# An expert stage rebuilt: batched gathers, expert outputs summed in PSUM, and weight splitting shared between three engines

## The reference

```python
combine = einsum('bske,bsk->bse', one_hot(expert_id, 16), p_g * top_p)
out = zeros_like(h)
for e in range(16):
    he = silu(h @ w_gate[e]) * (h @ w_up[e])        # 1024 -> 512
    out = out + combine[..., e:e + 1] * (he @ w_down[e])   # 512 -> 1024
x = x + out
```

## Time and profile before

| what | us |
|---|---|
| median of three runs | 1732.67 |
| the profiled execution: span from first to last instruction | 1733.3 |
| TensorE busy | 1584.7 (91%) |
| VectorE busy | 894.1 (52%) |
| ScalarE busy | 728.9 (42%) |
| GpSimd busy | 416.0 (24%) |

### The profile page before, as it was taken

One profiled execution on the slowest core, in us unless ns is written; L12 is line 12 of the kernel. 1 busy time (PEld: TensorE's weight loads), 2 busy tenths in 40 slices (PEclk: granted clock), 3 DMA queues, 4 the chain that ended last, 5 costly groups with the idle time before them and its releaser, 6 DMA issues. The chain is left out here.

```text
span 1733.3 us, 20738 instructions
## 1 busy us (share of the span) xinstructions
PE 1584.7 (91%) x6276; PEld 1251.4 (72%) x6276; DVE 894.1 (52%) x1403; ACT 728.9 (42%) x1033; POOL 416.0 (24%) x461
## 2 busy tenths in 40 slices
...
PEclk8998899997778788888879998999958888888877
...
GB/s 204 123 159 133 49 49 243 146 23 136 186 261 226 234 259 219 241 250 233 153 126 136 133 97 91 56 194 146 98 122 205 234 242 242 242 242 242 240 244 38
DMA packets 58345, 298.82 MB, mean 172 GB/s; under 512 B 4016, under 2 KB 8224, under 8 KB 45728
## 3 DMA queue, kind: packets, MB, share of 16 engines
...
## 5 line engine op out<-in xcount | busy, mean ns | idle before, releaser
L988 ACT ACTIVATE w_hi<-ring 128x1024 fp32r<-128x1024 f32 x424 | 424.9, 1057 | 27.9 <-PE bank L522 26.3
L1908 DVE TENSOR_TENSOR w_lo<-ring,w_hi 128x1024 fp32r<-128x1024 f32 x320 | 377.5, 1222 | 82.2 <-ACT w_hi L988 81.2
L1440 POOL TENSOR_TENSOR w_lo<-ring,w_hi 128x1024 fp32r<-128x1024 f32 x64 | 152.0, 2375 | 688.0 <-ACT w_hi L988 688.0
L863 PE MATMUL bank<-pick,h 128*128 128x64 f32 x1024 | 250.5, 419 | 3.7 <-DVE pick L1900 3.7
L863 PEld LDWEIGHTS bank<-pick,h 128*128 128x128 f32 x1024 | 249.3, 334 | 5.3 <-DVE pick L1900 3.9
L457 PE MATMUL bank<-ring,hT 128*128 128x512 f32 (+2 forms) x576 | 217.3, 538 | 4.0 <-ACT hT L1023 2.2
L892 PE MATMUL bank<-w_hi,ga 128*128 128x512 f32 x512 | 210.0, 410 | 3.8 <-DVE ga L1913 3.0
L893 PE MATMUL bank<-w_lo,ga 128*128 128x512 f32 x512 | 203.4, 397 | 0.0
L457 PEld LDWEIGHTS bank<-ring,hT 128*128 128x128 f32 x576 | 113.3, 199 | 101.7 <-issue 96.3
L939 PE MATMUL bank<-w_hi,hidT 128*128 128x512 f32 x256 | 142.1, 555 | 5.4 <-DVE hidT L1938 5.4
L940 PE MATMUL bank<-w_lo,hidT 128*128 128x512 f32 x256 | 133.6, 522 | 0.0
...
## 6 DMA issues: line engine op xcount, KB each, us to landing
ring<-in_w_e_gate SPq DMA_DIRECT2D x32, 2048.0 KB, 7.7
ring<-in_w_e_up SPq DMA_DIRECT2D x32, 2048.0 KB, 7.7
ring<-in_w_e_down SPq DMA_DIRECT2D x32, 2048.0 KB, 7.7
ring<-in_w_in SPq DMA_DIRECT2D x24, 2048.0 KB, 8.1
ring<-in_w_ckv SPq DMA_DIRECT2D x4, 2048.0 KB, 8.2
ring<-in_w_branch SPq DMA_DIRECT2D x4, 2048.0 KB, 10.4
ring<-in_w_out SPq DMA_DIRECT2D x4, 2048.0 KB, 10.4
ring<-in_w_cq SPq DMA_DIRECT2D x2, 2048.0 KB, 13.2
```

What stands on the lines that cost most here:

```text
L863: ins = mm(dst, h[:, tb, k::KD], pick[:, tb, 0, :], start=(tb == 0), stop=(tb == TB - 1))
L988: return A(dst, src, ACT.Copy, **kw)
L1440: g.tensor_tensor(w_lo[:, n % RP, :], ring[:, e_slot[j], 3 * PIECE:4 * PIECE], w_hi[:, n % RP, :].bitcast(F32), ALU.subtract).then_inc(sem ...
L1908: v.tensor_tensor(w_lo[:, n % RP, :], ring[:, e_slot[j], i * PIECE:i * PIECE + PIECE], w_hi[:, n % RP, :].bitcast(F32), ALU.subtract).then ...
```

## The change

The expert stage is rebuilt in these parts, the code of all other stages stays, but for the place of `hT` in SBUF and a few merged semaphores:

- **Gather.** The normed tokens `h` are split once a layer into `hs_hi` and `hs_lo` (ACT, DVE), and `pick` is made once for all 16 experts, as fp32r. One gather step is 4 matmuls with 256 columns (4 experts by 64 places) for one k of 8; the steps of the first group stand ahead of the turns, those of the next group are spread over the turns of the present one, two a turn. Both parts come out of the same bank, and one cast writes them to `ga` (ACT for even k, DVE for odd).
- **Fold.** ACT copies rows 64 to 127 of a gate or up bank to rows 0 to 63 of `gul` (`gl`, `ul`), DVE adds the other half from PSUM. silu and product are taken there, before the transposes: 4 matmuls by `ident` with 64 columns. The product also takes the token's weight `cw`, which comes out of the same two matmuls as `pickT` (`idc` holds the identity and the weights as high and low parts).
- **Scatter.** All experts are accumulated in four banks (`ACC`), and `x` is added to once at the end of the stage. `pickT` has two buffers; GpSimd copies its rows 0 to 63 to rows 64 to 127.
- **Splitting.** Pieces 0 to 2 of every chunk are ACT's and DVE's. Piece 3 of every chunk is GpSimd's alone, the cast to `w_hi` and the subtraction. SyncE waits for `w_lo` and `w_lo_p` itself.
- **Order.** The turns are written out one after the other, without a loop. The first gate chunk is split, and `hs_hi` and `hs_lo` are made, before the routing. The parameters of the next layer are issued by GpSimd behind its first piece.

```diff
+PER_TURN = dict(w_hi=9, w_lo=9, w_hi_p=3, w_lo_p=3, w_used=12, ga_mm=2, ga_ev_a=1, ga_ev_v=1,
+                pickT_mm=1, pickT=1, pickT_p=1, gu_cp=2, gu_sum=2, act_gate=1, hid=1,
+                hidT_mm=1, hidT_hi=1, hidT_lo=1, y_mm=1, y_hi=2, y_lo=2)
+PER_PASS = dict(pick=1, sc_mm=4, x_acc=4)
...
+GROUP = 4
+GROUPS = N_EXP // GROUP
+IDC = P + 2 * N_EXP
...
+SHARED_PIECES = (0, 1, 2)
...
+                def gather(b, g, k):
+
+                    for a, tok in enumerate((hs_hi, hs_lo)):
                         for tb in range(TB):
+                            ins = mm(bank[b][:, a * 256:a * 256 + 256], tok[:, tb, k, :],
+                                     pick[:, tb, GROUP * g:GROUP * g + GROUP, :].rearrange("p e c -> p (e c)"),
+                                     start=(tb == 0), stop=(tb == TB - 1))
...
+                            b = ACC[nh * 2 + tb]
+                            to = pickT[:, e % 2, tb * P:tb * P + P]
+                            mm(bank[b][:], to, y_hi[:, c], start=(e == 0), stop=False)
+                            ins = mm(bank[b][:], to, y_lo[:, c], start=False, stop=(e == N_EXP - 1))
+                            if e == N_EXP - 1:
+                                ins.then_inc(sem("sc_mm"), 1)
...
+                def turn(p, e):
+                    g, i = e // GROUP, e % GROUP
+
+                    pe.wait_ge(sem("ga_ev_a"), turns_before("ga_ev_a", l, p, 0) + min(N_EXP, GROUP * (g + 1)))
+                    pe.wait_ge(sem("ga_ev_v"), turns_before("ga_ev_v", l, p, 0) + min(N_EXP, GROUP * (g + 1) + i))
+                    widen(p, e, 0)
+
+                    if e > 0:
+                        pe.wait_ge(sem("y_lo"), turns_before("y_lo", l, p, e - 1) + 1)
+                    for tb in range(TB):
+                        ins = mm(bank[2][0:CAP, tb * IDC:tb * IDC + IDC], pick[:, tb, e, :], idc[:, tb, :],
+                                 start=True, stop=True)
+                    ins.then_inc(sem("pickT_mm"), 1)
+                    widen(p, e, 1)
+
+                    if g + 1 < GROUPS:
+                        pe.wait_ge(sem("gu_sum"), turns_before("gu_sum", l, p, e) + 1)
+                        gather(0, g + 1, 2 * i)
+                    if e > 0:
+                        scatter(p, e - 1)
+                    if g + 1 < GROUPS:
+                        pe.wait_ge(sem("ga_ev_a"), turns_before("ga_ev_a", l, p, 0) + GROUP * (g + 1) + i + 1)
+                        gather(0, g + 1, 2 * i + 1)
+
+                    pe.wait_ge(sem("hid"), turns_before("hid", l, p, e) + 1)
+                    q.settle()
...
+                        ins = tr(bank[1][:, t * CAP:t * CAP + CAP], hid[:, t::4], ident[0:CAP, 0:CAP])
+                    ins.then_inc(sem("hidT_mm"), 1)
...
+                def gathered(p, b, g, k):
+
+                    act.wait_ge(sem("ga_mm"), turns_before("ga_mm", l, p, 0) + g * KD + k + 1)
+                    copy(ga[:, g % 2, k].rearrange("p e a c -> p a e c"),
+                         bank[b][:].rearrange("p (a e c) -> p a e c", a=2, e=GROUP)).then_inc(sem("ga_ev_a"), 1)
...
+                    copy(gl, bank[0][CAP:P, :]).then_inc(sem("gu_cp"), 1)
...
+                    copy(pickT[0:CAP, e % 2, :].rearrange("p (t n) -> p t n", t=TB), both[:, :, 0:P])
+                    copy(cw_parts[0:CAP], both[:, :, P + e:IDC:N_EXP], accum_out=cw[0:CAP, :]).then_inc(sem("pickT"), 1)
+                    pieces(p, e, 2, (0,))
+                    act.wait_ge(sem("gu_sum"), turns_before("gu_sum", l, p, e) + 1)
+                    A(gl, gl, ACT.Silu).then_inc(sem("act_gate"), 1)
...
+                    copy(ul, bank[1][CAP:P, :]).then_inc(sem("gu_cp"), 1)
+                    if g + 1 < GROUPS:
+                        gathered(p, 0, g + 1, 2 * i)
...
+                pieces(0, 0, 0, SHARED_PIECES)
+                for tb in range(TB):
+                    act.wait_ge(sem("h_gained"), l * PER["h_gained"] + tb + 1)
+                    copy(hs_hi[:, tb], h[:, tb, :].rearrange("p (f k) -> p k f", k=KD)).then_inc(sem("hs_hi"), 1)
...
+                    pool.wait_ge(sem("w_used"), turns_before("w_used", l, p, e) + n + 1)
+                    q.settle()
+                    src = ring[:, s_, 3 * PIECE:4 * PIECE]
+                    g.tensor_copy(w_hi[:, n % RP, :], src).then_inc(sem("w_hi_p"), 1)
+                    pool.wait_ge(sem("w_hi_p"), turns_before("w_hi_p", l, p, e) + j + 1)
+                    q.settle()
+                    g.tensor_tensor(w_lo[:, n % RP, :], src, w_hi[:, n % RP, :].bitcast(F32),
+                                    ALU.subtract).then_inc(sem("w_lo_p"), 1)
+
+                def turn(p, e):
                     piece(p, e, 1)
+                    pool.wait_ge(sem("w_lo_p"), turns_before("w_lo_p", l, p, e) + LO_P_BIAS + 2)
+                    q.settle()
+                    pool.wait_ge(sem("pickT"), turns_before("pickT", l, p, e) + 1)
+                    q.settle()
+                    g.tensor_copy(pickT[CAP:P, e % 2, :], pickT[0:CAP, e % 2, :]).then_inc(sem("pickT_p"), 1)
+                    pool.wait_ge(sem("pickT_p"), turns_before("pickT_p", l, p, e) + 1)
+                    q.settle()
                     piece(p, e, 2)
...
+                piece(0, 0, 0)
+                for tb in range(TB):
+                    ins = g.tensor_copy(idc[:, tb, 0:P], ident[:])
+                ins.then_inc(sem("idc"), 1)
+                layer_parameters(bass.ds((L - 1) - l, 1))
...
+                pieces(0, 0, 0, SHARED_PIECES)
+                for tb in range(TB):
+                    dve.wait_ge(sem("hs_hi"), l * PER["hs_hi"] + tb + 1)
+                    v.tensor_tensor(hs_lo[:, tb], h[:, tb, :].rearrange("p (f k) -> p k f", k=KD),
+                                    hs_hi[:, tb].bitcast(F32), ALU.subtract).then_inc(sem("hs_lo"), 1)
...
+                def choose(p):
+
+                    first = p * N_EXP
                     for tb in range(TB):
+                        at = place[:, tb, first:first + N_EXP] if isinstance(first, int) else place[:, tb, bass.ds(first, N_EXP)]
+                        ins = v.tensor_tensor(pick[:, tb], bc(slot_no[:], [P, N_EXP, CAP]),
+                                              bc(at.unsqueeze(2), [P, N_EXP, CAP]), ALU.is_equal)
                     ins.then_inc(sem("pick"), 1)
...
+                def turn(p, e):
+                    g, i = e // GROUP, e % GROUP
+                    pieces(p, e, 1, SHARED_PIECES)
+                    dve.wait_ge(sem("gu_cp"), turns_before("gu_cp", l, p, e) + 1)
+                    v.tensor_tensor(gl, bank[0][0:CAP, :], gl, ALU.add).then_inc(sem("gu_sum"), 1)
+                    pieces(p, e, 2, (0,))
+                    dve.wait_ge(sem("gu_cp"), turns_before("gu_cp", l, p, e) + 2)
+                    v.tensor_tensor(ul, bank[1][0:CAP, :], ul, ALU.add).then_inc(sem("gu_sum"), 1)
+                    dve.wait_ge(sem("gu_sum"), turns_before("gu_sum", l, p, e) + 2)
...
+                    dve.wait_ge(sem("pickT"), turns_before("pickT", l, p, e) + 1)
+                    v.scalar_tensor_tensor(out=hid, in0=ul, scalar=cw[0:CAP, :], in1=gl,
+                                           op0=ALU.mult, op1=ALU.mult).then_inc(sem("hid"), 1)
+                    pieces(p, e, 2, (1,))
+                    if g + 1 < GROUPS:
+                        gathered(p, 0, g + 1, 2 * i + 1)
                     dve.wait_ge(sem("hidT_hi"), turns_before("hidT_hi", l, p, e) + 1)
+                    v.tensor_tensor(hidT[:, :, 1, :], bank[1][:, 0:4 * CAP].rearrange("p (t c) -> p t c", t=4),
+                                    hidT[:, :, 0, :].bitcast(F32), ALU.subtract).then_inc(sem("hidT_lo"), 1)
+                    pieces(p, e, 2, (2,))
+                    if e < N_EXP - 1:
+                        pieces(p, e + 1, 0, SHARED_PIECES)
...
+                        v.tensor_tensor(xv, bank[ACC[n]][:], xv, ALU.add).then_inc(sem("x_acc"), 1)
```

More of the change, by code:

```diff
@@ L73, in split_piece_used @@
     return LAST_USE[SPLIT[n // 4]] if n % 4 == 3 else ("dw_used", 3 * (n // 4) + n % 4 + 1)
-PER_TURN = dict(split=3, w_hi=12, w_lo=10, w_lo_p=2, w_used=12, pick=1, pickT_mm=1, pickT=1, ga_mm=1, ga_hi=1,
-                ga_lo=1, gu_sb=2, guT_mm=2, act_gate=1, hid=1, hidT_hi=1, hidT_lo=1,
-                y_mm=1, y_hi=2, y_lo=2, sc_mm=4, x_acc=4)
+PER_TURN = dict(w_hi=9, w_lo=9, w_hi_p=3, w_lo_p=3, w_used=12, ga_mm=2, ga_ev_a=1, ga_ev_v=1,
+                pickT_mm=1, pickT=1, pickT_p=1, gu_cp=2, gu_sum=2, act_gate=1, hid=1,
+                hidT_mm=1, hidT_hi=1, hidT_lo=1, y_mm=1, y_hi=2, y_lo=2)
+PER_PASS = dict(pick=1, sc_mm=4, x_acc=4)
 CAP = 64
@@ L255, in trunk @@
         most = sb("most", [P, 2])
-        sb("between", [P, (late - size["over"]) // 4 + 16])
+        assert size["over"] >= late
         w_hi = sb("w_hi", [P, RP, PIECE], F32R)
@@ L261, in trunk @@
         hT_lo = sb("hT_lo", [P, KD, S], F32R)
+        hs_hi, hs_lo = (t[:].rearrange("p k s -> p (k s)").rearrange("p (t k f) -> p t k f", t=TB, k=KD)
```

(14 more changed lines are left out.)

361 lines of the change are left out of this document (140 added, 221 removed).

## The result

| kernel | median us | runs | ratio to the kernel before (95% interval) |
|---|---|---|---|
| before | 1732.69 | 4 | 1 |
| changed | 1618.28 | 4 (1617.76 to 1624.06) | 0.935 (0.9333 to 0.9368) |

The change takes 6.5% off. The forecast was 1650 in a range of 1590 to 1730: sign and range held, the point was 32 us too high.

A forecast was written before the change was run, and what follows sets the result against it. TensorE bounds the kernel before; after, a serial GpSimd and VectorE stream of 21.7 us a turn, turn 23.3. Gain 48.5 less head 7 is 41.5 a layer, 83 in all: 1733.3 to 1650 us, range 1590 to 1730.

The forecast's parts named there:

- TensorE is the bound before and not after: Expert turn: TensorE's issue sets the 26.1 us before; its need falls from 24.9 to 15.6 us.
- VectorE and GpSimd keep each other out: Expert turn: two-SBUF-input VectorE instructions and SBUF-reading GpSimd instructions exclude each other, a serial stream of 21.7 us.
- the forecast's signs: Expert stage: GpSimd and VectorE together near 95% busy, split subtractions often 2 to 3.5 us, TensorE near 70% busy.
- The stream of 21.7 us is a floor, the turn 1.6 above it: Expert turn: GpSimd 10.6, VectorE subtractions 10.4 and `hid` 0.65 run serially; walked through, the turn is 23.3 us.
- A2: Theory formed after the first four runs: VectorE's own work, time kept out and waits set the turn.
- Gate start to last down end, 368 us: Expert stage of a layer: 16 x 23.3 = 373, minus 3 and 2, against 416.6 before; gain 48.5.
- Head +7 us a layer: Before the first gate matmul: later routing, choosing and batched gather cost 7 us, from +2 to +12.
- Tail the same: Last down matmul to end of the adds, 861.5 to 866.0 before, keeps its form.
- GpSimd's cast 1.04 us: GpSimd's splitting of piece 3: a 1024-column cast into fp32r takes 1.04 us, from the plain COPY row.
- The break-even rival: GpSimd's cast slower: no gain from 1.9 us; at 2.37 the turn is 27.3, the kernel 1778; chance 0.15.
- the walk: One expert turn followed instruction by instruction, with exclusion and waits of 2 to 2.5 us: 23.3 us.
- The low clock (chance 0.08): Rival: TensorE falls to the low level in its gaps; down alone adds 3.1 us a turn, kernel 1749; chance 0.08.

The follow-up runs named there:

- g11_fill_both: Changed kernel with the second down subtraction moved ahead of the up addition on VectorE and its cast ahead of the gate activation on ScalarE: 1618.7 us.
- e1_castact: Changed kernel with GpSimd's three casts a turn moved to ScalarE, GpSimd keeping its three subtractions: 1649.2 us, turn 23.9.
- e3_memset: Changed kernel with GpSimd filling piece 3 with constants instead of splitting it: total 2299.9 us not usable (other routing in layer 2), layer 1 turn mean 16.8.
- e6_one: As e2_no_gpsimd, but GpSimd makes one subtraction a turn and VectorE 11: 1532.8 us, turn 19.8.
- g12_cast_only: As e2_no_gpsimd, but GpSimd makes the three casts of a turn's fourth pieces: 1527.8 us, turn 19.2.
- e2_no_gpsimd: Changed kernel with GpSimd out of the splitting, VectorE making all 12 subtractions and ScalarE all 12 casts a turn: 1506.3 us, turn 18.6.
- e8_acc: Changed kernel with the sum over experts in PSUM undone, VectorE adding four banks to x every turn: 1693.8 us, turn 24.7.
- e7_fill: Changed kernel with the second down subtraction moved ahead of the up addition on VectorE only: 1683.9 us, turn 24.1.
- g10_ga_act: As e2_no_gpsimd, with hs_lo and VectorE's third piece behind the routing and odd gather evacuations moved to ScalarE: 1499.7 us, turn 18.6.

## Why the prediction was right, and where it was off

- *TensorE is the bound before and not after.* Right: 91% busy, then 80%, and 17.1 us of a turn of 22.2, with waits for w_lo. I had put its need at 15.6. The difference is about the 1.6 us at the low level; in the turns of g11_fill_both that stay at 1.00 TensorE is busy for 15.7.
- *VectorE and GpSimd keep each other out.* Right, and the strongest term. Shown by e3_memset (no SBUF input, no effect), e6_one and e1_castact (2.1 us on VectorE for each GpSimd subtraction) and g12_cast_only (0.4 for each cast). One or the other of the two engines is busy for 99% of the nine turns, the 95% of the forecast's signs. How much is lost depends on what meets: three subtractions and three casts cost 5.0 us in the changed kernel, not 7.5.
- *The stream of 21.7 us is a floor, the turn 1.6 above it.* This is the step that was off. The turn is 22.2, not 23.3: 1.1 us in each of 32 turns would be 35 us; 29 of it show between the forecast's 368 us a layer and the measured 353.6, since the first turns are longer, and the point was 32 off. The floor was no floor, since g11_fill_both has turns of 20.63 with the same operations, and shortening the stream by 3.1 us made the turn longer (e1_castact). Its terms were also too large: at 2.1 us for a subtraction and 0.4 for a cast the stream is 10.4 + 0.65 + 6.3 + 1.2 = 18.6 us, an estimate. What the runs show in its place is a ring through VectorE's queue. For the changed kernel: 14.4 own, 9 x (1.71 - 1.22) + 0.6 for `hid` = 5.0 kept out, 2.8 of waits, 22.2 together. For e1_castact: 14.7 + 6.2 + 3.0 = 23.9. For e2_no_gpsimd: 17.9 + 0.7 = 18.6. Own time, time kept out and waits always add up to the turn, so this is an account, and a forecast only where the waits are known: A2 gave the numbers of e6_one, g12_cast_only and e8_acc, and missed e7_fill, g11_fill_both and g10_ga_act, where ScalarE's queue is as late. That the turn came out inside the range while the floor behind it was wrong is in part luck.
- *Gate start to last down end, 368 us.* Measured 353.6 (451.12 to 804.74); before 416.6. *Head +7 us a layer:* the first gate matmul is 6.3 later. In it the two `hs_lo`, taken at 1.16 us each, cost 2.0 each and were kept out besides (6.0 together), and the first gather took 5.5 us, not 7. *Tail the same:* yes, 4.2 us against 4.5. So 63.0 - 6.3 = 56.7 a layer, 113 in all, against 111 between the profiled spans (forecast 83).
- *GpSimd's cast 1.04 us.* Right: the shortest is 1.037 us. The break-even rival (1.9 us) matches the mean of 1.89, but that is 1.04 and the time kept out, which the walk had counted already. `pickT` on GpSimd is 1.0 us beside VectorE, 0.39 when alone.
- *The low clock (chance 0.08).* Half true: each of the nine turns has a low stretch (mean clock 0.92), in one turn in the last two up pieces, in the next in half of down, which the rival named. Each is 1.6 us of TensorE's time, half of the rival's 3.1. The waits of 2 us ahead of the up pieces were in my walk, and I took the high level for them; ahead of down the wait is 1.4. What it costs the turn was not measured apart.
- *A slip in the sum of before.* 56 x 0.23 is 12.9; the 13.1 goes with 0.235. Nothing hangs on it.
- *DMA hidden.* Right: 284 GB/s, and no wait of the nine turns ends on a transfer.
- *The rule of the Trainium skill* (SBUF — State Buffer, Who interferes with whom) held: VectorE's subtraction takes up to 3.4 us beside GpSimd's operations that read SBUF and 1.22 beside its fills. It is what speaks against a quarter of the splitting on GpSimd. I used it for the floor and didn't draw the last consequence: undoing that part alone gives 112 us, about as much as the whole change had brought (114).
